# A bf16 encoder block on eight cores: six staging slots for W_ff1, early table loads, and a replanned instruction order

## The reference, cut to what matters

```python
proj = jnp.einsum('bsd,de->bse', x, w_in[l])            # (8, 8192, 1792)
q, k, v, gu, gv = jnp.split(proj, SPLITS, axis=-1)      # 512, 128, 128, 512, 512
attn = banded_window_attention(q, k, v, sink[l])        # |t - s| <= 128, 8 heads, ALiBi, sink
gu = jax.nn.gelu(gu, approximate=False)
gv = jax.nn.gelu(gv, approximate=False)
sgu = gu * (einsum('gts,bnsgc->bntgc', w_s, layer_norm(gv)) + b_s)   # per 128 positions
mixed = jnp.concatenate([rms_norm(attn), rms_norm(sgu)], axis=-1)
x = layer_norm(ALPHA * x + mixed @ w_out)
h = jnp.square(jax.nn.relu(x @ w_ff1))                  # 1024 -> 4096
x = layer_norm(ALPHA * x + h @ w_ff2)                   # 4096 -> 1024
```

## Time and profile before

| | us |
|---|---|
| median of 3 runs | 2870.37 (2736.93 to 3171.15) |
| the profiled execution, slowest core | 2747.33 |
| its span, first to last instruction (core 2) | 2745.7 |
| spans of cores 0 to 3 | 2743.4, 2741.4, 2745.7, 2743.5 |
| spans of cores 4 to 7 | 2727.3, 2729.5, 2726.5, 2727.7 |
| TensorE busy (core 2) | 2628.2 |
| VectorE, ScalarE, GpSimd busy (core 2) | 1391.5, 1091.1, 662.8 |

### The profile page before, as it was taken

One profiled execution on the slowest core, in us unless ns is written; L12 is line 12 of the kernel. 1 busy time (PEld: TensorE's weight loads), 2 busy tenths in 40 slices (PEclk: granted clock), 3 DMA queues, 4 the chain that ended last, 5 costly groups with the idle time before them and its releaser, 6 DMA issues.

```text
span 2745.7 us, 55945 instructions; the slowest of 8 cores (2726.5 to 2745.7 us)
## 1 busy us (share of the span) xinstructions
PE 2628.2 (96%) x20122; PEld 1684.9 (61%) x20332; DVE 1391.5 (51%) x2562; ACT 1091.1 (40%) x1853; POOL 662.8 (24%) x941
## 2 busy tenths in 40 slices
PE   4679999999999999999999999999999999999998
PEld 2347776776777677677777777864444444444443
DVE  5776667677667767767667673112122221122213
ACT  3345555655656565565656654520001100011000
POOL 1331212212112211211111111113234332344323
PEclk8789999999999999999999999999999999999987
DMA  8764434433433443343443336873445334354332
GB/s 257 223 158 120 110 103 112 117 97 109 124 109 101 112 117 105 105 120 103 116 116 96 116 102 150 180 192 123 141 166 177 130 129 163 138 184 146 132 107 77
DMA packets 181474, 362.53 MB, mean 132 GB/s; under 512 B 79696, under 2 KB 79696, under 8 KB 172112
## 3 DMA queue, kind: packets, MB, share of 16 engines
q1 hardware_dynamic: 141488, 224.97, 25.1%
q10 hardware_dynamic: 16528, 91.76, 9.9%
q0 software_dynamic: 23184, 42.22, 9.5%
HBM read 216.54 MB, written 150.99 MB: 134 GB/s over the span
## 4 chain that ended last, share of the span: by engine, by line
PE 90%; issue 2%; DVE 2%; DMA 2%; ACT 2%; POOL 1%; SPq 0%; DVEq 0%; POOLq 0%; ACTq 0%
PE psum L867 32%; PE psum L829 30%; PE psum L782 8%; PE psum L681 4%; PE psum L695 4%; PE psum L697 4%; PE psum L738 2%; PE psum L751 2%; PE psum L906 1%; DMA arena<-w_gu 1%; PE psum L776 1%; PE psum L687 1%; PE psum L689 1%; DMA arena<-w_ff 1%; PE psum L713 1%
## 5 line engine op out<-in xcount | busy, mean ns | idle before, releaser
L829 PE MATMUL psum<-arena 128*128 128x256 bf16 x8192 | 983.6, 273 | 4.1 <-ACT arena L833 1.5
L867 PE MATMUL psum<-arena 128*128 128x512 bf16 x3888 | 878.1, 384 | 5.7 <-DVE arena L874 0.9
L829 PEld LDWEIGHTS psum<-arena 128*128 128x128 bf16 x8192 | 771.3, 98 | 141.7 <-issue 42.4
L867 PEld LDWEIGHTS psum<-arena 128*128 128x128 bf16 x3968 | 390.0, 99 | 493.0 <-issue 58.1
L833 ACT ACTIVATE arena<-psum 128x512 f32<-128x512 f32 x512 | 302.9, 593 | 296.5 <-PE psum L829 287.7
L669 POOL TENSOR_SCALAR arena<-arena 128x1 f32<-128x1 f32 x320 | 78.1, 244 | 1405.2 <-DVE arena L880 462.5
L884 ACT ACTIVATE arena<-arena 128x1024 f32<-128x1024 f32 x62 | 77.0, 1241 | 814.3 <-DVE arena L882 441.4
L874 DVE SCALAR_TENSOR_TENSOR arena<-psum,arena 128x512 f32<-128x512 f32 x124 | 85.8, 692 | 614.3 <-PE psum L867 544.0
L747 ACT ACTIVATE arena<-arena 128x512 bf16<-128x512 f32 x380 | 231.6, 626 | 202.0 <-DVE arena L744 166.3
L744 DVE SCALAR_TENSOR_TENSOR arena<-psum,arena 128x512 f32<-128x512 f32 x380 | 249.1, 678 | 7.8 <-PE psum L738 7.1
L782 PE MATMUL psum<-arena 128*128 128x512 bf16 x960 | 226.5, 388 | 14.1 <-DVE arena L779 6.8
(11 more groups left out here) (84 smaller groups left out, 2030.0 us busy)
## 6 DMA issues: line engine op xcount, KB each, us to landing
hsc<-arena SPq DMA_DIRECT2D x256, 256.0 KB, 2.3
arena<-hsc ACTq DMA_DIRECT2D x58, 1024.0 KB, 5.2
arena<-x SPq DMA_DIRECT2D x64, 512.0 KB, 4.8
x1s<-arena SPq DMA_DIRECT2D x64, 512.0 KB, 2.7
out<-arena SPq DMA_DIRECT2D x31, 1024.0 KB, 4.8
arena<-x1s ACTq DMA_DIRECT2D x29, 1024.0 KB, 5.4
arena<-xt POOLq DMA_DIRECT2D x64, 256.0 KB, 5.0
arena<-w_ff SPq DMA_DIRECT2D x32, 512.0 KB, 5.5
```

The costliest lines, as they stand in the source:

```text
L829: R.pe(lambda e, fc=fc, ph=ph, z=z: [e.matmul(ph.ap[:, z * 256:(z + 1) * 256], lhsT=w1q[fc // 4].ap[:, c, (fc % 4) * 128:(fc % 4 + 1) * 12 ...
L867: R.pe(lambda e, s_=s_, q=q: [e.matmul(ps[s_][hf].ap, lhsT=hb[fc // 16].ap[:, fc % 16, s_ * 128:(s_ + 1) * 128], rhs=w2c[fc // 4].ap[:, fc ...
```

## The change

- `load_w1` gets six slots: `w1st[1]`, `w1st[2]`, and the two halves each of `w1q[7]` and `w1q[6]`, the last parts of W_ff1 to be filled. `w1st[0]`, the memory of `x1T[0]`, is no slot any more. Pieces 24 to 27 use four slots, 28 to 31 two.
- The casts of W_ff1 go in turn to ScalarE, VectorE, ScalarE, GpSimd (16, 8 and 8 pieces; before 0, 22 and 10).
- W_out uses the first four of the same slots, and every second piece is cast on ScalarE (4 of 8).
- The copy of q out of PSUM (L684) is done on ScalarE for blocks 0 to 6. In `ff1(0)` and `ff1(1)` both squares are on ScalarE.
- When the planner switches ScalarE's table, it puts an activation of one element ahead, in the stream directly after the operation before; it depends only on a memset.
- The planner's durations and the constant `HOP` are changed, and with them the order of all engines.
- In `ff2`, the residual buffer is tracked by its two 128-position halves instead of as one.
- The loop that starts FF1 early ends at NI - 3 instead of NI.

```diff
-HOP = 80.0
+HOP = 140.0
 TBL = 1283.0
+TINY = 190.0
...
-    return sum((c / 2.4 + 2.5) if c >= 128 else 31.0 for c in cols)
+    return sum((c / 2.4 + (4.0 if c > 256 else 5.5)) if c >= 128 else 31.0 for c in cols)
...
-    return 230.0 + 0.833 * n
+    return 180.0 + 0.85 * n
...
-            if e == "act" and o.tbl is not None:
+            if e == "act" and o.tbl is not None and o.tbl != tblstate[0]:
+
+                w = Op()
+                w.eng, w.fn, w.is_dma, w.signal, w.ticket, w.sem, w.semval = "act", self.warm[o.tbl], False, False, None, None, None
+                w.dur, w.tbl, w.lat, w.idx, w.tag, w.v, w.nbytes = TINY, o.tbl, 0.0, o.idx, o.tag, o.v, 0
+                w.alldeps = {self.warm_dep}
...
+                streams[e].append(w)
                 tblstate[0] = o.tbl
...
+    s67 = [[Buf(w1q[q].ap.rearrange("p c n -> p (c n)")[:, h * 2048:(h + 1) * 2048].bitcast(F32), f"st{q}{h}") for h in range(2)] for q in (6, 7)]
+    slots = w1st[1:] + s67[1] + s67[0]
...
+    def cast(k, rd, wr, out, src):
+        if k % 4 == 1:
+            R.dve(lambda e: e.tensor_copy(out=out, in_=src), rd, wr, 1024, 2)
+        elif k % 4 == 3:
+            R.pool(lambda e: e.tensor_copy(out=out, in_=src), rd, wr, 512)
+        else:
+            R.act(lambda e: e.activation(out=out, in_=src, func=AF.Copy), rd, wr, 1024)
...
-        sg = w1st[k % NX1]
+        j = (k + 4) % 6 if k < 24 else (k % 4 if k < 28 else k % 2)
+        sg = slots[j]
...
-        st = wost[c % 4]
+        st = slots[c % 4]
...
-        R.dve(lambda e: e.tensor_copy(out=dst.ap, in_=pq.ap), [pq], [dst, gate[b]], 512)
+        if b < 7:
+            R.act(lambda e: e.activation(out=dst.ap, in_=pq.ap, func=AF.Copy), [pq], [dst, gate[b]], 512)
+        else:
+            R.dve(lambda e: e.tensor_copy(out=dst.ap, in_=pq.ap), [pq], [dst, gate[b]], 512)
...
-                if k == 0:
+                if k == 0 and i > 1:
...
-                    in1=yo.ap[:, s_, hf * 512:(hf + 1) * 512], op0=ALU.mult, op1=ALU.add), [ps[s_][hf], yo], [yo], 512)
+                    in1=yo.ap[:, s_, hf * 512:(hf + 1) * 512], op0=ALU.mult, op1=ALU.add), [ps[s_][hf], yl_], [yl_], 512)
...
-        while fn < NI and 2 * fn + 3 + lag(fn) <= b:
+        while fn < NI - NHXT and 2 * fn + 3 + lag(fn) <= b:
```

More of the change, by code:

```diff
@@ L525, in build_nc @@
     x1r.append(over("x1r2", F32, [2, D]))
+    x1rh = [[Buf(x_.ap[:, s_, :], f"x1rh{i}_{s_}") for s_ in range(2)] for i, x_ in enumerate(x1r)]
     if verbose:
@@ L559, in build_nc @@
     R.dve(lambda e: e.memset(mhalf.ap, -0.5), [], [mhalf], 1)
+    wscr = small("wscr", 2)
+    R.warm_dep = R.dve(lambda e: e.memset(wscr.ap, 0.0), [], [wscr], 1)
+    R.warm = {t: (lambda e, f=f: e.activation(out=wscr.ap[:, 1:2], in_=wscr.ap[:, 0:1], func=f)) for t, f in (("el", AF.Exp), ("gelu", AF.Gelu))}
     R.dve(lambda e: e.memset(epsB.ap, EPS / (ALPHA * ALPHA)), [], [epsB], 1)
@@ L577, in build_nc, with slot_extra @@
     wp = [0]
+    s67 = [[Buf(w1q[q].ap.rearrange("p c n -> p (c n)")[:, h * 2048:(h + 1) * 2048].bitcast(F32), f"st{q}{h}") for h in range(2)] for q in (6, 7)]
+    slots = w1st[1:] + s67[1] + s67[0]
+    fresh = [False] * 6
+    def slot_extra(j):
+        if j >= 2 and not fresh[j]:
+            fresh[j] = True
+            return [w1q[7 if j < 4 else 6]]
+        return []
+    def cast(k, rd, wr, out, src):
[5 more added lines that the diff above has]
+            R.act(lambda e: e.activation(out=out, in_=src, func=AF.Copy), rd, wr, 1024)
     def load_w1():
@@ L583, in load_w1 @@
         q, r = divmod(k, 4)
[L584 removed]
+        j = (k + 4) % 6 if k < 24 else (k % 4 if k < 28 else k % 2)
+        sg = slots[j]
         flat = w1q[q].ap.rearrange("p c n -> p (c n)")
         sl = slice(r * 1024, (r + 1) * 1024)
[L587 to L592 removed]
+        R.dma("sp", lambda e: e.dma_start(out=sg.ap, in_=w_ff1[q][:, sl]), [], [sg] + slot_extra(j), f"w1st{j}", 600000)
+        rd, wr = ([sg], [w1p[k], w1q[q]] + (s67[q - 6] if q >= 6 else [])) if r == 0 else ([sg, w1q[q]], [w1p[k]])
+        cast(k, rd, wr, flat[:, sl], sg.ap)
     x_load(0)
@@ L659, in build_nc @@
     for c in range(8):
-        st = wost[c % 4]
+        st = slots[c % 4]
         R.dma("sp", lambda e, c=c, st=st: e.dma_start(out=st.ap, in_=w_out[c * 128:(c + 1) * 128, :]),
-              [], [st], f"stage{c % 4}", 524288)
-        R.dve(lambda e, c=c, st=st: e.tensor_scalar(out=w_out_bf[c].ap, in0=st.ap, scalar1=gcol.ap[:, c:c + 1],
-                                                    scalar2=None, op0=ALU.mult), [st, gcol], [w_out_bf[c]], 1024, 2)
+              [], [st] + slot_extra(c % 4), f"w1st{c % 4}", 600000)
+        if c % 2 == 0:
+            R.act(lambda e, c=c, st=st: e.activation(out=w_out_bf[c].ap, in_=st.ap, func=AF.Copy, scale=gcol.ap[:, c:c + 1]),
+                  [st, gcol], [w_out_bf[c]], 1024)
+        else:
+            R.dve(lambda e, c=c, st=st: e.tensor_scalar(out=w_out_bf[c].ap, in0=st.ap, scalar1=gcol.ap[:, c:c + 1],
+                                                        scalar2=None, op0=ALU.mult), [st, gcol], [w_out_bf[c]], 1024, 2)
     small_dma("m_g1", G1, G1.ap, ln1_g.partition_broadcast(128), 524288)
@@ L668, in rsqrt @@
     def rsqrt(src_ap, src_buf, eps, outb):
-        R.pool(lambda e: e.tensor_scalar(out=outb.ap, in0=src_ap, scalar1=eps, scalar2=None, op0=ALU.add), [src_buf], [outb], 50)
-        R.pool(lambda e: e.tensor_tensor(out=outb.ap, in0=outb.ap, in1=mhalf.ap, op=ALU.pow), [outb, mhalf], [outb], 50)
+        R.pool(lambda e: e.tensor_scalar(out=outb.ap, in0=src_ap, scalar1=eps, scalar2=None, op0=ALU.add), [src_buf], [outb], 90)
+        R.pool(lambda e: e.tensor_tensor(out=outb.ap, in0=outb.ap, in1=mhalf.ap, op=ALU.pow), [outb, mhalf], [outb], 290)
     def front(b):
@@ L806, in ff1_x @@
             R.dma("sp", lambda e, m=m, dst=dst: e.dma_start_transpose(out=dst.ap, in_=x1h[m * 128:(m + 1) * 128, :]),
-                  [x1h_lt[m]], [dst, xgate[i]], f"x1T{i % NX1}_{s_}", 262144)
+                  [x1h_lt[m]], [dst, xgate[i]], f"x1T{i % NX1}_{s_}", 380000)
     hn = [0]
@@ L865, in ff2 @@
         for s_ in range(2):
+            yl_ = x1rh[i % 3][s_]
             for q in range(8):
@@ L884, in ff2 @@
             R.act(lambda e, s_=s_, p=p: e.activation(out=yo.ap[:, s_, :], in_=yo.ap[:, s_, :], func=AF.Identity,
-                                                     bias=nmrB[p].ap, scale=rstdB[p].ap), [yo, nmrB[p], rstdB[p]], [yo], 1024)
+                                                     bias=nmrB[p].ap, scale=rstdB[p].ap), [yl_, nmrB[p], rstdB[p]], [yl_], 1024)
             aff = R.pool
             aff(lambda e, s_=s_: e.tensor_tensor(out=yo.ap[:, s_, :], in0=yo.ap[:, s_, :], in1=G2.ap, op=ALU.mult),
-                [yo, G2], [yo], 1024)
+                [yl_, G2], [yl_], 1024)
             aff(lambda e, s_=s_: e.tensor_tensor(out=yo.ap[:, s_, :], in0=yo.ap[:, s_, :], in1=B2.ap, op=ALU.add),
-                [yo, B2], [yo], 1024)
+                [yl_, B2], [yl_], 1024)
         R.dma("sp", lambda e: e.dma_start(out=out[i * 256:(i + 1) * 256, :].rearrange("(s p) d -> p s d", p=128), in_=yo.ap),
-              [yo], [], f"out{i % 3}", 1048576)
+              x1rh[i % 3], [], f"out{i % 3}", 1048576)
     def ff2_last(i):
@@ L901, in ff2_last @@
             p = s_
-            yh = [Buf(yo.ap[:, s_, hf * 512:(hf + 1) * 512], f"yh{s_}{hf}", extra=[yo.lt] if s_ == 0 and hf == 0 else []) for hf in range(2)]
+            yh = [Buf(yo.ap[:, s_, hf * 512:(hf + 1) * 512], f"yh{s_}{hf}") for hf in range(2)]
             for hf in range(2):
```

36 lines of the change are left out of this document (17 added, 19 removed).

## The result

| | before | changed |
|---|---|---|
| runs of the comparison, us | 2732.84, 2736.93 (all four: median 2803.65, to 3171.15) | 2705.36 to 2708.67, median 2707.15 |
| ratio | | 0.9895 [0.9876, 0.9915] |
| spans of the eight cores, profiled execution | 2726.5 to 2745.7 | 2699.9 to 2703.8 |
| core 5's span in both profiled executions | 2729.5 | 2703.8 |

The change makes the kernel 1.05% faster, 28 to 29 us of some 2735. Executions whose slowest core lay more than 1.5% above the fastest of the same kernel, or one of whose dies was over 1% longer at a lower granted clock, are left out of every comparison here. In the profile of before, cores 0 to 3 are 16 us longer than cores 4 to 7 by their medians (core 2 has a clock of 0.83 from 2600 us on); that made the forecast's base too high. Core 5, without that stretch, went from 2729.5 to 2703.8.

What follows compares the result with a forecast made beforehand. TensorE bounds the kernel, losing 99.3 us in the first 180. Loss there falls to 73.9 (25.4 won), plus 4 for tables, less 2 for ScalarE's waits: 27.4, from 2745.7 to 2718.3, with 1.6 outside 2720 us; range 2690 to 2766.

Steps and rivals of the forecast that it cites:

- FF1 is held by `x1T`, and that wait ends last: Start: FF1 begins only at 172.20 us because the x1T buffers serve as W_ff1's slots; the change removes this wait.
- 10.7 us from a block's store to FF1, so 126.0: Start: 10.7 us from store to first FF1 matmul, added to block 1's store at 115.29, gives 126.0 us.
- 7 us for VectorE's relief by block 1: Start: 11.9 us of VectorE work gone by block 1's store; 7 taken, so ff1(0) starts at 119 us.
- Pieces at 2.5 us each, the last at 142: W_ff1 loads: six slots bring a piece every 2.5 us instead of 3.0, the last about 142 us.
- The rival of the pieces that come no faster: W_ff1 loads: last piece stays about 157, some 12 us lost in ff1(0)'s last groups, 2732 us; chance 0.15.
- 88% from there on: From 119 to 180 us: TensorE taken as 88% busy because of ScalarE's load, 7.3 us lost.
- Early tables, 4 us, nothing after 300: Table switches: six in the start save at most 7.7 us of latency, 4 taken; nothing counted later.
- ScalarE's waits for pieces, 2 us: Start: ScalarE casts waiting for their DMA hold Exp and what is queued behind; counted as 2 us lost.
- The rival on the other side: Start: 20 new ScalarE casts wait for late pieces, 2.5 us each, 50 in all, 2768 us; chance 0.10.
- The new order, 0: Replanned order, mainly from 300 us: 0, bounds -8 and +27; rival that it costs 27, 2747 us, chance 0.15.
- The freed VectorE: Rival: blocks go at a freed VectorE's pace, TensorE 95% busy after, 13 and some 10 more, 2697 us; chance 0.15.
- FF2's halves, 0: FF2's residual step: tracking the halves apart gains 0, as the wait was over before the matmuls were.

Runs made afterwards that it cites:

- x1: The changed kernel run again as yardstick, nothing altered: 2703.06, 2705.20 and 2708.45 us, ratio 0.9899 to the kernel before.
- x2: Changed kernel with the transposed load of FF1 0's input again waiting until all 32 W_ff1 pieces are cast: 2721.7 us beside 2705.2.
- x9: Kernel before with only the six W_ff1 slots, four of them for W_out; its own casts, durations and late table loads: ratio 0.9962.
- x13: Kernel before with the six slots and the early table loads, its own casts and durations: ratio 0.9888.
- x7: Changed kernel planned with the durations, HOP and byte counts of before: 2702.6 and 2705.2 us, ratio 0.9866.
- x6: Changed kernel with W_ff1 and W_out casts, q copies and FF1's first squares distributed as before, back on VectorE: 2707.2 and 2709.7 us.
- x4: Changed kernel with the two halves of w1q[6] and w1q[7] tracked apart as slots: 2700.5 and 2701.1 us beside 2705.2.
- x10: Changed kernel with W_ff1 going through four slots instead of six: 2708.2 us, ratio 0.9912.
- x5: Kernel before, in its own order, with only the one-element activations for early table loads added: 2720.6 us beside 2732.8.
- x3: Changed kernel without the one-element activations, every engine's order the same: 2727.7 us beside 2705.2.
- x8: Kernel before planned with the new durations, HOP and byte counts and nothing else: 2739.4 us, ratio 1.0013.
- x11: Changed kernel with slots tracked apart and the durations of before: 2696.5, 2698.3 and 2701.2 us beside 2736.7, ratio 0.9862.

## Why the prediction came out as it did

The forecast change was 27.4 us and 28 were measured; the time was put at 2720 us and was 2707. Two steps failed. The first is the base, the 2745.7 us from which the sum starts: 2747.3 was an execution with a low clock on one die from 2600 us on, and the kernel's level is 2733. I saw the stretch and left it in "as some core had such a stretch". The timed runs of before show that most executions compared don't have it (nine on x1's chip lie at 2731.24 to 2736.89). With 2733.5 as the base the same sum gives 2706, so almost all of the 13 us are the base. The second is the term for the early tables, 4 us in the start and nothing after 300: they gave 12 us alone, and TensorE was busy 7 us longer after 300. That the change came out right all the same is luck, since the slots and casts were put too high by about as much. Nor is 2% "about what a measurement of this kernel can tell": the interval of the ratio is 0.2% to either side.

Step by step:

- *FF1 is held by `x1T`, and that wait ends last.* Right. x2 puts it back and loses 16.5 us.
- *10.7 us from a block's store to FF1, so 126.0.* Wrong. The first FF1 of before needs blocks 0 and 1, whose `x1h` had long landed; the 10.7 us counted from block 3's store had nothing of block 3 in them. For block 1 the landing of `x1h` comes first: its transpose goes out 121.42 - 114.02 = 7.4 us after the store, and FF1 began 20.8 us after it.
- *7 us for VectorE's relief by block 1.* It can't be seen there: block 1 was stored at 114.02, and at 113.88 before. Two effects met, and the sum had only one of them. In the order of before the slots alone put block 1 back by 9 us (median of the cores 123.5 in x9 and 123.4 in x13, 114.4 in before); why, no run settles. With the casts and copies moved as well and the same planned lengths it is back at 112.9 (x7), so there the relief is worth 10.5 us; with the new lengths it is 0.7 (114.7 in x6, 114.0 in the changed kernel). Part of what the slots cost is W_out held back by the shared tracker: in x4 block 1 comes at 106.33 on core 5.
- *Pieces at 2.5 us each, the last at 142.* Wrong: 158. The rival of the pieces that come no faster was right in this, but its price of 12 us wasn't paid: TensorE was busy 98% from 140 on, since FF1 takes its weights group by group. The number of slots hardly matters (x10). What sets the pace instead is argued and not shown: from 30 to 165 us SyncE's queue stood 40 us for x1's stores and `x1h`, but the DMA engines were also busy 0.94 of 60 to 120 us, and no run tells the two apart.
- *88% from there on.* Too low: 98% from 140 to 180 us. A late start and a dense follow-up made up for each other: 21 us of work more in 120 to 180 was forecast, 19 came. That is luck too.
- *Early tables, 4 us, nothing after 300.* The largest miss in the mechanism. 12 us alone (x5), 22 in the changed kernel (x3). I argued from TensorE's 98.6%, and didn't join the 19.1 us that it did lose to what stood in the same trace: 6.0 us in ten waits of L713, behind VectorE, GpSimd's rsqrt and Gelu. x5 gave back 7.1 us there. The sentence that the trace has no drain behind the load holds in the changed kernel too; a load and its one-element activation, and Gelu behind it:

```profile
114.33 1.28 ACT L574 ACT_TABLE_LOAD   x1
115.63 0.20 ACT L574 ACTIVATE arena<-arena 128x1 f32<-128x1 f32 x1
115.74 0.58 ACT L737 ACTIVATE arena<-psum 128x512 f32<-128x512 f32 x1
```

  Gelu starts 1.41 us after the load did. The added activation takes 0.20 us, not up to 0.625. The Trainium skill, "ScalarE: Activation LUTs", section "What ACT_TABLE_LOAD costs", puts a load and a drain at 2.66 us; the measured 1.41 us leaves no room for the drain here either. The 12 us of x5 come from the order of a load and a wait, by its rows of idle time above. Why the same edit is worth 22 us in the changed kernel isn't shown; x3 loses a part of it in every steady block (26.76 us for 26.52), which the order of before doesn't.
- *ScalarE's waits for pieces, 2 us.* ScalarE stood 3.9 us in two waits for W_ff1 from 40 to 180 us and 2.9 for W_out; what of this reached TensorE no run separates, though its waits for Exp grew by 5.5 us. The rival on the other side (2.5 us a cast, 50 in all) didn't come: with the casts back on VectorE (x6) the kernel isn't faster.
- *The new order, 0.* Within its bounds: alone it costs 4 to 7 us (x8, the interval just touching none), in the changed kernel 1 to 2 (x7, x11), so that rival wasn't idle.
- *The freed VectorE.* Its 95% was nearer than the 88%, and GpSimd's rsqrt step in the start did get shorter (0.70 us, 0.81 on core 5 of before), but the blocks didn't come sooner.
- *FF2's halves, 0.* Off by 2.5 us. My ground was that the wait "was over before the matmuls were", and core 2 does show nothing at the last FF2. Core 5 of before shows TensorE waiting 1.9 us for L889 at the last FF2, a row of a core that I hadn't read.

So slots and first casts were put too high by some 10 us (23.4 forecast, 10 to 13 in x9), early tables too low by 8, and the sum came out by that.
